# A chunked RWKV-7 inverse: accumulated in PSUM, transposed by VectorE in 32x32 blocks, two pairs' chains interleaved

## The chip, the cores and the metric

One core of a Trainium2 chip runs the whole program. The metric is the device time of one execution in microseconds; the times of before are the median of three runs with their lowest and highest. Lower is better.

## The reference

The program is one inference step of a two-layer hybrid decoder (D_MODEL 1024) in fp32, for one prompt of 256 tokens and eight samples of one token each. Each layer has a SwiGLU half (width 2816), a projection into three groups (RWKV-7, a short convolution, Mamba-2), a projection w_out back, and a second SwiGLU half. The change touches the RWKV-7 group alone. It has 16 heads of 64, and per token and head

```python
Sa = einsum('bhij,bhj->bhi', S, -kk_t)
S  = S * w_t[:, :, None, :] + Sa[..., None] * b_t[:, :, None, :] + v_t[..., None] * k_t[:, :, None, :]
y  = einsum('bhij,bhj->bhi', S, r_t)
```

The kernel does the prompt in four chunks of C = 64 tokens. Inside a chunk the coupling through Sa is a triangular system: with N the strictly lower 64x64 matrix of products between the tokens' b and kk vectors (each with its decay), X = (I - N)^-1 is needed for every head and chunk. The inverse is built by doubling: blocks of 2, and then for b in LEVELS = (2, 4, 8, 16, 32) the part of N that couples neighbouring blocks of size b, N_b, is taken in by X <- X + X N_b X. After level b, X consists of blocks of 2b on the diagonal.

## The kernel before

The eight samples and the prompt's tokens lie together as 264 columns. FFN and projection products stream weights from HBM, split in a high and a low fp32r half by ScalarE and VectorE or GpSimd (`Stream`, lines 154 to 236), three products per piece on TensorE.

`back_stage` (line 1574) holds the recurrence, w_out and the second FFN. It handles the 16 heads as RT = 8 pairs. A pair's four chunks of two heads are a tile of 128 partitions (two halves of 64) x 4 x 64. For a pair p the steps are:

- `decays` (ScalarE) and `weigh` (GpSimd, four multiplications) make the operands; `gram` (TensorE, line 2170) multiplies them into PSUM banks 3 and 4; `mask` (VectorE, line 1996) masks them into `gm`; `turn` and `tokens` bring transposed operands.
- `first` on GpSimd (line 1759) takes the first level out of gm into `xt`, the transpose of X; `start` (VectorE, line 2002) adds the identity. `turn_x` (TensorE, line 2192) multiplies it by the identity into PSUM bank 0, and `x_copy` (ScalarE, line 1809) makes `x` of it.
- Five levels i. `level` (GpSimd, line 1731) cuts N_b out of gm. `level_t1` (TensorE) forms N_b X in bank 0, `t1_copy` (ScalarE) brings it to `t1`, and `level_u` (TensorE) forms two products: X N_b X (bank 1, for levels 0 to 3) and its transpose (bank 2). `update` (VectorE, line 2007) adds the first to x and the second to xt, with x in SBUF. Each product is `blocks` (line 2186): eight matrix products of 64x64, sixteen instructions.
- `gv`, `solve` (line 2236, needs the finished xt), `transfer`, `own_outputs`, `own_states` and `chunk` carry the state through the four chunks; `mean_of`, `variance_of`, `centre`, `gated` normalise.
- `step(m, 0..7)` on VectorE does the recurrence of the eight samples for pair m; its rows come by DMA from `row_scratch`, its state by SyncE's queue.

Every engine has its own hand-written order in a loop `for g in range(RT + 2)`; all meet through counting semaphores. In a round g before, pair g gets gram, masks, start and turn_x; pair l = g - 1 gets all five levels, one behind the other; pair c = g - 2 gets solve, transfer, outputs and states; pair p = g - 3 gets its normalisation. Between the levels stand the other pairs' steps as filling. In rounds 8 and 9 the filling is the w_out product of the convolution groups, `short(mt)`: 24 products each; ScalarE there does the splits of w_out (`ws.split_hi`) and in round 8 the logarithm and exponential of five variances, with table loads. ScalarE also issues the stores of the final states (line 1838) and of the shift rows. VectorE has fillings too: in rounds 0 to 3 two bonus operations each (line 2112), in rounds 0 and 1 three and five scalings (line 2117). SyncE loads and stores the samples' rows and states and, from pair 6 on, w_out.

Of the kernel before, what the change touches and what calls it, by code (L numbers as in the profile page):

```python
# [22 lines left out]
P = 128  # L23
# [1550 lines left out]
def back_stage(nc, env, mix, layer, d):  # L1574
# [15 lines left out]
    with Stage(nc, f"back{layer}") as st:  # L1590
# [15 lines left out]
        t1 = st.sb("n_x", [P, 4, C])  # L1606
# [28 lines left out]

        def load_row(e, m, n):
# [4 lines left out]
        T1B, UB, GB, WB, EB = 0, 1, 3, 5, 6  # L1641
# [30 lines left out]
        with nc.Block() as block:  # L1672
# [42 lines left out]
            def _(pool):  # L1715
# [15 lines left out]
                def level(p, i):  # L1731
                    n = LV * p + i
# [18 lines left out]
                for g in range(RT + 1):  # L1751
                    l = g - 1
                    if l >= 0:
                        level(l, 1)
# [6 lines left out]
                    if l >= 0:  # L1761
                        level(l, 2)
                    if g + 1 < RT:
                        weigh(g + 1)
                    if l >= 0:
                        level(l, 3)
                    if g == RT - 1:
                        for q in range(3):
                            short_split_lo(q)
                    if g == RT:  # L1770
                        ws.split_lo(pool, 2)
                    if l >= 0:
                        level(l, 4)
                        key_row(l)
                    if g == RT - 1:
                        short_split_lo(3)
                    if g < RT:
                        level(g, 0)
# [7 lines left out]
            def _(act):  # L1786
# [15 lines left out]
                def t1_copy(p, i):  # L1802
                    n = LV * p + i
                    act.wait_ge(s("t1_ps"), n + 1)
                    if n:
                        act.wait_ge(s("ut_ps"), n)
                    act.activation(t1[:].rearrange("p q t -> p (q t)"), ps[:, T1B, 0:4 * C], ACT.Copy).then_inc(s("t1_in"), 1)  # L1807
# [73 lines left out]
                for i in range(2):  # L1881
                    act.activation(rows[0:V * NS].rearrange("p v b j -> p (v b j)")[:, i * 512:(i + 1) * 512],
                                   ps[0:V * NS, UB + i, :], ACT.Copy).then_inc(s("turned"), 1)
                act.activation(cend[:], mix.cum[:, :, :, C], ACT.Exp, scale=-DECAY).then_inc(s("cend"), 1)
                act.wait_ge(s("cend"), 1)
                for g in range(RT + 2):
                    l, c, p = g - 1, g - 2, g - 3
                    if g + 1 < RT:
                        decays(g + 1)
                    if 0 <= l < RT:  # L1890
                        t1_copy(l, 0)
                    if g == 1:
                        shift_rows(3)
                    if c >= 0:
                        uw_copy(c)
                    if c >= 1:
                        final_copy(c - 1)
                    if g == RT:
# [4 lines left out]
                    if g == RT + 1:  # L1903
                        ws.split_hi(act, 4)
                        ws.split_hi(act, 5)
                    if 0 <= l < RT:
                        t1_copy(l, 1)
# [4 lines left out]
                    if g < RT:  # L1912
                        tokens(g, 0)
                    if g < 2:
# [6 lines left out]
                    if 0 <= l < RT:  # L1921
                        t1_copy(l, 2)
# [3 lines left out]
                    if p >= 0:  # L1926
                        square(p)
                    if g == RT + 1:
                        ws.split_hi(act, 6)
                    if c >= 0:  # L1930
                        state_copy(c, 0)
                    if 0 <= l < RT:
                        t1_copy(l, 3)
# [3 lines left out]
                    if g < RT:  # L1937
                        tokens(g, 1)
                    if g == RT:
                        ws.split_hi(act, 3)  # L1940
                    if p >= 0:
                        variance(p)
                    if c >= 0:
                        state_copy(c, 1)
                    if 0 <= l < RT:
                        t1_copy(l, 4)
                        rv_copy(l)
# [9 lines left out]
                    if g < RT:  # L1957
                        x_copy(g)
# [36 lines left out]
            def _(dve):  # L1995
# [11 lines left out]
                def update(p, i):  # L2007
                    four = lambda b: ps[:, b, 0:4 * C].rearrange("p (q t) -> p q t", q=4)
                    if i < LV - 1:
                        dve.wait_ge(s("u_ps"), (LV - 1) * p + i + 1)  # L2010
                        if i:
                            dve.wait_ge(s("x_up"), (LV - 1) * p + i)
                        else:
                            dve.wait_ge(s("x_in"), p + 1)
                        dve.tensor_tensor(x[:, p % 2], x[:, p % 2], four(UB), ALU.add).then_inc(s("x_up"), 1)
                    dve.wait_ge(s("ut_ps"), LV * p + i + 1)
                    if i:
                        dve.wait_ge(s("xt_up"), LV * p + i)
                    dve.tensor_tensor(xt[:, p % 3], xt[:, p % 3], four(UB + 1), ALU.add).then_inc(s("xt_up"), 1)
# [62 lines left out]

                for g in range(RT + 2):
                    l, c, p = g - 1, g - 2, g - 3
                    if g < RT:
                        mask(g, 0)
                        mask(g, 1)
                    if 0 <= l < RT:
                        update(l, 0)
                        step(l, 0)  # L2090
# [4 lines left out]
                    if 0 <= l < RT:  # L2095
                        update(l, 1)
                        step(l, 1)
                        step(l, 2)
                        update(l, 2)
# [412 lines left out]
```

## Time and profile before

| | us |
|---|---|
| median of 3 runs | 1666.39 (1666.23 to 1671.9) |
| span of the profiled execution | 1667.1 |
| TensorE busy | 1566.2 |
| VectorE, ScalarE, GpSimd busy | 1140.1, 858.5, 262.7 |
| gram(0) to the last state copy, layer 0 | 441.2 to 597.0 |

The profiled execution's own time is its span, 0.7 us above the median. TensorE's busy time counts each matrix product to its modelled end, so products that wait for one another in a pipeline look like full work. In the windows below the columns are the stretch, its length, the busy time of TensorE (PE), its weight loads (PEld), VectorE (DVE), ScalarE (ACT) and GpSimd (POOL) with numbers of records, the granted TensorE clock (1.00 is 2.4 GHz), the DMA engines' busy share and GB/s. A timeline row is start, length, engine, line, operation, output and inputs, count, and in brackets the idle time before it with what ended it.

### The profile page before, as it was taken

Reading aid. Unit: us, or ns where it says so; the run is one execution under the profiler, and the core shown is the slowest. Engines: PE = TensorE matmul, PEld = TensorE weight load, DVE = VectorE, ACT = ScalarE, POOL = GpSimd, SP = SyncE. Lnnn points to the kernel's source line nnn. Section 1 sums busy time; section 2 is a strip of 40 time slices with the busy share of each in tenths; the row PEclk is TensorE's granted clock in tenths of the full one; section 3 lists DMA queues with packets and bytes.
Section 4 is the critical chain, followed back from the end, with each engine's and each line's share of the span. In section 5 each row is a group of like instructions: output and inputs, shape, how many; then the busy total and the mean of one; then the engine's idle time right before and its main releaser. Section 6 shows DMA issues by size and latency. Waiting matters only on the chain. (4 is left out here: it accounts for less than half of the span.)

```text
span 1667.1 us, 41414 instructions
## 1 busy us (share of the span) xinstructions
PE 1566.2 (94%) x17379; PEld 1486.8 (89%) x17379; DVE 1140.1 (68%) x1822; ACT 858.5 (51%) x1515; POOL 262.7 (16%) x259
## 2 busy tenths in 40 slices
PE   7999999989799899999999999999997989899997
PEld 6999999987688789999999999989775878799997
DVE  6565587795798667665575656968768886676654
ACT  5444464667444555444354444657673445554443
POOL 0000003001356431000000000030014554300000
PEclk9999999999899999999999999999998999999999
DMA  7555556471244545555454655644703463455552
GB/s 230 178 172 170 168 159 199 130 208 53 59 125 120 144 157 161 194 179 186 143 186 160 194 183 175 189 141 128 215 1 102 126 178 98 131 189 187 183 178 71
DMA packets 280650, 256.28 MB, mean 154 GB/s; under 512 B 48054, under 2 KB 268700, under 8 KB 280450
## 3 DMA queue, kind: packets, MB, share of 16 engines
q1 hardware_dynamic: 276698, 252.05, 48.5%
q8 instruction: 139, 2.28, 0.6%
q10 hardware_dynamic: 3768, 1.59, 0.4%
q14 instruction: 45, 0.37, 0.1%
HBM read 242.22 MB, written 11.38 MB: 152 GB/s over the span
## 5 line engine op out<-in xcount | busy, mean ns | idle before, releaser
L209 ACT ACTIVATE front_hi<-front_raw 128x1024 fp32r<-128x1024 f32 (+2 forms) x230 | 238.5, 1039 | 262.0 <-PE ps L234 255.5
L216 DVE TENSOR_TENSOR front_lo<-front_raw,front_hi 128x1024 fp32r<-128x1024 f32 (+1 forms) x210 | 252.2, 1201 | 109.0 <-ACT front_hi L209 108.2
L209 ACT ACTIVATE out_hi<-out_raw 128x1024 fp32r<-128x1024 f32 (+1 forms) x168 | 173.3, 1038 | 219.1 <-PE ps L234 205.1
L216 DVE TENSOR_TENSOR out_lo<-out_raw,out_hi 128x1024 fp32r<-128x1024 f32 (+1 forms) x148 | 183.9, 1243 | 108.1 <-ACT out_hi L209 107.3
L232 PE MATMUL ps<-front_h_hi,front_hi 128*128 128x264 f32 (+1 forms) x816 | 241.3, 296 | 4.9 <-DVE front_lo L216 3.3
L234 PE MATMUL ps<-front_h_hi,front_lo 128*128 128x264 f32 (+1 forms) x816 | 233.0, 286 | 0.0
L233 PE MATMUL ps<-front_h_lo,front_hi 128*128 128x264 f32 (+1 forms) x816 | 232.7, 285 | 0.0
L232 PE MATMUL ps<-ffn_h_hi,out_hi 128*128 128x264 f32 x704 | 200.7, 285 | 0.1
L233 PE MATMUL ps<-ffn_h_lo,out_hi 128*128 128x264 f32 x704 | 200.0, 284 | 0.0
L234 PE MATMUL ps<-ffn_h_hi,out_lo 128*128 128x264 f32 x704 | 199.8, 284 | 0.0
L232 PE MATMUL ps<-in_h_hi,front_hi 128*128 128x264 f32 x688 | 197.4, 287 | 0.0
L234 PE MATMUL ps<-in_h_hi,front_lo 128*128 128x264 f32 x688 | 196.5, 286 | 0.0
L233 PE MATMUL ps<-in_h_lo,front_hi 128*128 128x264 f32 x688 | 196.5, 286 | 0.0
L232 PEld LDWEIGHTS ps<-front_h_hi,front_hi 128*128 128x128 f32 (+1 forms) x816 | 154.1, 189 | 13.5 <-issue 12.7
L233 PEld LDWEIGHTS ps<-front_h_lo,front_hi 128*128 128x128 f32 (+1 forms) x816 | 154.2, 189 | 0.7
L234 PEld LDWEIGHTS ps<-front_h_hi,front_lo 128*128 128x128 f32 (+1 forms) x816 | 153.5, 188 | 0.1
L216 POOL TENSOR_TENSOR front_lo<-front_raw,front_hi 128x1024 fp32r<-128x1024 f32 (+1 forms) x20 | 50.1, 2504 | 543.9 <-ACT front_hi L209 543.9
L232 PEld LDWEIGHTS ps<-ffn_h_hi,out_hi 128*128 128x128 f32 x704 | 132.7, 189 | 0.4 <-ACT ffn_h_hi L283 0.2
L233 PEld LDWEIGHTS ps<-ffn_h_lo,out_hi 128*128 128x128 f32 x704 | 132.7, 188 | 0.1
L234 PEld LDWEIGHTS ps<-ffn_h_hi,out_lo 128*128 128x128 f32 x704 | 132.6, 188 | 0.0
L233 PEld LDWEIGHTS ps<-in_h_lo,front_hi 128*128 128x128 f32 x688 | 131.3, 191 | 0.1
L232 PEld LDWEIGHTS ps<-in_h_hi,front_hi 128*128 128x128 f32 x688 | 131.2, 191 | 0.1
(400 smaller groups left out, 3891.7 us busy)
## 6 DMA issues: line engine op xcount, KB each, us to landing
front_raw<-in_w_in SPq DMA_DIRECT2D x50, 1024.0 KB, 5.2
out_raw<-in_ffn_w_in SPq DMA_DIRECT2D x44, 1024.0 KB, 5.2
front_raw<-in_ffn_w_in SPq DMA_DIRECT2D x40, 1024.0 KB, 5.3
back_sample_rows<-row_scratch SPq DMA_DIRECT2D x160, 128.0 KB, 3.0
out_raw<-in_w_out SPq DMA_DIRECT2D x16, 1024.0 KB, 6.3
front_raw<-in_ffn_w_out SPq DMA_DIRECT2D x16, 896.0 KB, 4.6
out_raw<-in_ffn_w_out SPq DMA_DIRECT2D x16, 896.0 KB, 4.6
front_raw<-in_ffn_w_out SPq DMA_DIRECT2D x8, 1024.0 KB, 5.0
```

The costliest lines, as they stand in the source:

```text
L209: act.activation(self.hi[n % self.RING][:, 0:k, 0:w], self._raw(n), ACT.Copy).then_inc(self.hi_ready, 1)
L216: eng.tensor_tensor(self.lo[n % self.RING][:, 0:k, 0:w], self._raw(n), self.hi[n % self.RING][:, 0:k, 0:w].bitcast(F32), ALU.subtract).the ...
L232: pe.matmul(out, hi[:, j, 0:w], x_hi[:, j], start=start and j == 0, stop=False)
L233: pe.matmul(out, hi[:, j, 0:w], x_lo[:, j], start=False, stop=False)
L234: mm = pe.matmul(out, lo[:, j, 0:w], x_hi[:, j], start=False, stop=stop and j == k - 1)
```

## The change

1. X is accumulated in PSUM. `turn_x` starts an accumulation in bank 1 or 2 (by the pair's parity) and leaves it open; `level_u` of levels 0 to 3 adds X N_b X there, and `x_copy(p, i)` copies the bank to `x` before each level. The additions to x on VectorE are gone.
2. xt for levels 1 to 4 is `dve.transpose` of x, in 32x32 blocks. The second product of `level_u` is left for level 4 alone; one addition (`finish`) takes it into xt.
3. Levels 0, 1 and 2, 3, 4 of neighbouring pairs share a round: in round g pair g does levels 0 and 1, and pair b = g - 1 levels 2, 3 and 4, in the order (b,2) (g,0) (b,3) (g,1) (b,4) on TensorE. `t1` has two buffers.
4. start and turn_x stand at the beginning of pair g's own round; gram and masks of pair g + 1 towards its end, behind (b,4). The other steps are set into new places. Ahead of the loops stand gram(0), its masks and the first three shift turns.

```diff
-                def update(p, i):
-                    four = lambda b: ps[:, b, 0:4 * C].rearrange("p (q t) -> p q t", q=4)
-                    if i < LV - 1:
-                        dve.wait_ge(s("u_ps"), (LV - 1) * p + i + 1)
...
-                        dve.tensor_tensor(x[:, p % 2], x[:, p % 2], four(UB), ALU.add).then_inc(s("x_up"), 1)
-                    dve.wait_ge(s("ut_ps"), LV * p + i + 1)
...
-                    dve.tensor_tensor(xt[:, p % 3], xt[:, p % 3], four(UB + 1), ALU.add).then_inc(s("xt_up"), 1)
+                def turn_blocks(p, i):
+                    flat = lambda a: a.rearrange("p q t -> p (q t)")
+                    dve.wait_ge(s("x_in"), copied[p, i])
+                    dve.transpose(flat(xt[:, p % 3]), flat(x[:, p % 2])).then_inc(s("xt_in"), 1)
+
+                def finish(p):
+                    dve.wait_ge(s("u_ps"), order_of[p, 4] + 1)
+                    dve.tensor_tensor(xt[:, p % 3], xt[:, p % 3], ps[:, XB + p % 2, 4 * C:8 * C].rearrange("p (q t) -> p q t", q=4),
+                                      ALU.add).then_inc(s("xt_up"), 1)
...
-                def x_copy(p):
-                    act.wait_ge(s("x_ps"), p + 1)
-                    act.activation(x[:, p % 2].rearrange("p q t -> p (q t)"), ps[:, T1B, 0:4 * C], ACT.Copy).then_inc(s("x_in"), 1)
+                def x_copy(p, i):
+                    if i:
+                        act.wait_ge(s("u_ps"), order_of[p, i - 1] + 1)
+                    else:
+                        act.wait_ge(s("x_ps"), p + 1)
+                    act.activation(x[:, p % 2].rearrange("p q t -> p (q t)"), ps[:, XB + p % 2, 0:4 * C], ACT.Copy).then_inc(s("x_in"), 1)
...
+                def level_u(p, i):
+                    n = order_of[p, i]
+                    pe.wait_ge(s("t1_in"), n + 1)
                     if i:
+                        pe.wait_ge(s("xt_in"), turned_blocks(p, i))
+                    if i < LV - 1:
+                        blocks(XB + p % 2, 0, xt[:, p % 3], t1[:, n % 2], False, i == LV - 2).then_inc(s("u_ps"), 1)
                     else:
...
+                        blocks(XB + p % 2, 4 * C, t1[:, n % 2], xt[:, p % 3]).then_inc(s("u_ps"), 1)
```

TensorE's order in a round after the change, from the diff (b = g - 1, c = g - 2, p = g - 3): t1(b,2), solve(c), turn_final(c-1), [short(2)], turn_x(g), u(b,2), t1(g,0), turn(g,0), [short(0)], transfer(c), mean_of(p), u(g,0), t1(b,3), turn(g,1), own_outputs(c), u(b,3), t1(g,1), own_states(c), variance_of(p), [short(1)], u(g,1), t1(b,4), chunk(c,1), gram(g+1), gv(b), chunk(c,2), u(b,4), chunk(c,3). The shorts are those of rounds 8 and 9.

VectorE's: start(g), turn_blocks(b,3), step(b,0), transfer(c), turn_blocks(g,1), step(b,1), centre(p), step(b,2), turn_blocks(b,4), step(b,3), gated(p), turn_blocks(g,2), fillings, step(b,4), mask(g+1) twice, step(b,5), finish(b), step(b,6), step(b,7).

ScalarE's: t1_copy(b,2), uw_copy(c), final_copy(c-1) with its store, x_copy(g,0), x_copy(b,3), decays(g+1), t1_copy(g,0), [shift rows 0 to 2 in round 0], tokens(g,0), x_copy(g,1), [shift store], t1_copy(b,3), tokens(g,1), square(p), x_copy(b,4), t1_copy(g,1), state_copy(c,0), variance(p), x_copy(g,2), t1_copy(b,4), the other state copies. In round 8 the logarithm block stands behind x_copy(b,3).

GpSimd's: first(g), level(g,0), level(b,3), weigh(g+1), level(g,1), [short splits in round 7], level(b,4), key_row(b), level(g,2).

## Rows read from the trace of the kernel before

**Rows 1.** The page, part 1: busy time, share of the span, instructions.
```profile
PE 1566.2 (94%) x17379; PEld 1486.8 (89%) x17379; DVE 1140.1 (68%) x1822; ACT 858.5 (51%) x1515; POOL 262.7 (16%) x259
```

**Rows 2.** Windows of layer 0: length, busy us (records) by engine, clock, DMA share, GB/s.
```profile
450.45:467.31 16.86, 13.95 (x335) 11.97 (x335) 15.52 (x28) 6.42 (x18) 8.86 (x11) 1.00 0.38 124
...
497.24:511.64 14.40, 14.05 (x426) 12.57 (x424) 13.29 (x26) 6.58 (x20) 9.17 (x11) 1.00 0.48 134
...
543.90:562.02 18.12, 14.23 (x409) 12.71 (x406) 13.45 (x25) 8.65 (x24) 10.85 (x10) 1.00 0.96 270
...
562.02:582.87 20.85, 18.52 (x420) 16.77 (x416) 12.33 (x22) 13.09 (x22) 9.86 (x7) 1.00 0.11 31
...
467.31:543.90 76.59, 72.50 (x2164) 65.64 (x2160) 67.17 (x123) 33.84 (x99) 45.52 (x55) 1.00 0.45 125
```

**Rows 3.** Timeline of two half levels, layer 0, fifth round.
```profile
514.03 0.68 PE L2189 MATMUL ps<-back_inverse,back_n_levels 64*64 64x64 f32 x16
...
514.44 0.64 ACTq L1838 DMA_DIRECT2D out_p_wkv<-back_final_state  x1
...
515.18 0.38 ACT L1807 ACTIVATE back_n_x<-ps 128x256 f32<-128x256 f32 x1 [0.77 <-PE ps L2189]
...
515.61 0.68 PE L2189 MATMUL ps<-back_n_x,back_inverse_t 64*64 64x64 f32 x16 [0.36 <-ACT back_n_x L1807]
...
516.13 0.63 PE L2189 MATMUL ps<-back_inverse_t,back_n_x 64*64 64x64 f32 x16
```

**Rows 4.** Waits of 449 to 600 us: total us, times, longest us.
```profile
ACT back_n_x L1807 <- PE ps L2189: 21.5, 26, 2.7
...
PEld ps L2189 <- issue: 9.0, 18, 2.9
```

**Rows 5.** Groups by line over the span: xcount | busy us, mean ns | idle before.
```profile
L2189 PE MATMUL ps<-back_inverse,back_n_levels 64*64 64x64 f32 x1280 | 54.3, 222 | 7.5 <-issue 6.2 <-ACT back_inverse L1811 0.7
...
L2189 PE MATMUL ps<-back_inverse_t,back_n_x 64*64 64x64 f32 x1280 | 53.1, 220 | 3.3 <-issue 3.2
...
L2189 PE MATMUL ps<-back_n_x,back_inverse_t 64*64 64x64 f32 x1024 | 44.0, 225 | 9.4 <-ACT back_n_x L1807 9.1
...
L2019 DVE TENSOR_TENSOR back_inverse_t<-back_inverse_t,ps 128x256 f32<-128x256 f32 x80 | 33.4, 418 | 7.1 <-PE ps L2189 4.7
...
L1807 ACT ACTIVATE back_n_x<-ps 128x256 f32<-128x256 f32 x80 | 30.5, 381 | 45.6 <-PE ps L2189 44.8
...
L2015 DVE TENSOR_TENSOR back_inverse<-back_inverse,ps 128x256 f32<-128x256 f32 x64 | 26.8, 419 | 26.4 <-PE ps L2189 25.8
...
L1871 ACT ACTIVATE shift_new_rows<-ps 9x512 f32<-9x512 f32 (+1 forms) x14 | 7.7, 564 | 2.4 <-PE ps L2345 2.0
```

**Rows 6.** Timeline of VectorE, two additions back to back.
```profile
498.43 0.41 DVE L2015 TENSOR_TENSOR back_inverse<-back_inverse,ps 128x256 f32<-128x256 f32 x1
498.76 0.41 DVE L2019 TENSOR_TENSOR back_inverse_t<-back_inverse_t,ps 128x256 f32<-128x256 f32 x1
```

**Rows 7.** Timeline, start of the stage in layer 0.
```profile
443.25 1.29 DVE L1998 TENSOR_TENSOR back_products<-ps,cst 128x512 f32<-128x512 f32 x2 [5.15 <-PE ps L2182]
...
446.33 0.68 PE L2198 MATMUL ps<-cst,back_inverse_t 64*64 64x64 f32 x16 [0.23 <-DVE back_inverse_t L2004]
```

**Rows 8.** Timeline of the eighth round, layer 0.
```profile
565.47 0.37 PE L232 MATMUL ps<-short_hi,out_hi 128*128 128x264 f32 x1
...
566.68 1.28 ACT L1900 ACT_TABLE_LOAD   x1 [0.66 <-ACT back_final_state L1836]
...
570.69 1.31 ACT L1860 ACTIVATE xs<-xs 128x1320 f32<-128x1320 f32 x1
...
571.29 0.28 PE L234 MATMUL ps<-short_hi,out_lo 128*128 128x264 f32 x1
```

**Rows 9.** Line 2039 on VectorE: shortest, median, longest ns.
```profile
L2039 DVE TENSOR_TENSOR back_prod<-back_sample_wkv,back_sample_rows x16: 684/980/1267, 452.5 to 1388.1; 128x512 f32<-128x512 f32 x16
```

**Rows 10.** Windows of TensorE ahead of the stage, clock in the last but two columns.
```profile
436.00:438.00 2.00, 0.01 (x1) 0.50 0.00 0
```

More of the change, by code:

```diff
@@ L1634, in back_stage, with turned_blocks @@
         M0, R0, G0, Y0 = 0, P, 2 * P, 3 * P
+        order_of = {}
+        for g in range(RT + 1):
+            order = [(g - 1, 2), (g, 0), (g - 1, 3), (g, 1), (g - 1, 4)]
+            for pair, i in order:
+                if 0 <= pair < RT:
+                    order_of[pair, i] = len(order_of)
+        copied = {}
+        for g in range(RT + 1):
+            for pair, i in [(g, 0), (g - 1, 3), (g, 1), (g - 1, 4), (g, 2)]:
+                if 0 <= pair < RT:
+                    copied[pair, i] = len(copied) + 1
+        def turned_blocks(p, i):
+            return sum(1 for (pair, j), n in copied.items() if j and n <= copied[p, i])
         def load_row(e, m, n):
@@ L1777, in _ @@
                     if g < RT:
-                        level(g, 0)
+                        level(g, 2)
                     if g == RT - 1:
@@ L1895, in _ @@
                         uw_copy(c)
+                    if g == RT + 1:
+                        ws.split_hi(act, 4)
+                        ws.split_hi(act, 5)
                     if c >= 1:
                         final_copy(c - 1)
+                    if g < RT:
+                        x_copy(g, 0)
+                    if 0 <= b < RT:
+                        x_copy(b, 3)
+                    if g and g + 1 < RT:
+                        decays(g + 1)
                     if g == RT:
@@ L2081, in y_split_lo @@
                     dve.tensor_tensor(y_lo[:, p], r[:, p], y_hi[:, p].bitcast(F32), ALU.subtract).then_inc(s("y_lo"), 1)
+                mask(0, 0)
+                mask(0, 1)
                 for g in range(RT + 2):
-                    l, c, p = g - 1, g - 2, g - 3
+                    b, c, p = g - 1, g - 2, g - 3
                     if g < RT:
[L2086 to L2090, printed above, removed]
+                        start(g)
+                    if 0 <= b < RT:
+                        turn_blocks(b, 3)
+                        step(b, 0)
                     if g == RT + 1:
@@ L2108, in _ @@
                     if g < RT:
-                        start(g)
+                        turn_blocks(g, 2)
                     if g < 4:
@@ L2118, in _ @@
                                                  op0=ALU.mult, op1=ALU.mult).then_inc(s("short_scaled"), 1)
-                    if 0 <= l < RT:
-                        step(l, 5)
-                        update(l, 4)
-                        step(l, 6)
-                        step(l, 7)
+                    if 0 <= b < RT:
+                        step(b, 4)
+                    if g + 1 < RT:
+                        mask(g + 1, 0)
+                        mask(g + 1, 1)
+                    if 0 <= b < RT:
+                        step(b, 5)
+                        finish(b)
+                        step(b, 6)
+                        step(b, 7)
                     if g == RT - 1:
@@ L2184, in gram, with blocks @@
                     mm.then_inc(s("g_ps"), 1)
-                def blocks(at, left, right):
+                def blocks(bank, at, left, right, start=True, stop=True):
                     for q in range(4):
                         for w in half:
-                            mm = pe.matmul(ps[w, at, q * C:(q + 1) * C], left[w, q], right[w, q], start=True, stop=True)
+                            mm = pe.matmul(ps[w, bank, at + q * C:at + (q + 1) * C], left[w, q], right[w, q], start=start, stop=stop,
+                                           skip_group_check=not start)
                     return mm
@@ L2400, in _ @@
                         shift_turn(6)
-                    if 0 <= l < RT:
-                        level_t1(l, 3)
-                    if g < RT:
-                        turn(g, 1)
                     if p >= 0:
                         variance_of(p)
-                    if 0 <= l < RT:
-                        level_u(l, 3)
+                    if g == RT:
+                        short(1)
+                    if g < RT:
+                        level_u(g, 1)
+                    if 0 <= b < RT:
+                        level_t1(b, 4)
                     if c >= 0:
                         chunk(c, 1)
-                    if 0 <= l < RT:
-                        level_t1(l, 4)
-                        gv(l)
+                    if g + 1 < RT:
+                        gram(g + 1)
+                    if 0 <= b < RT:
+                        gv(b)
                     if g == RT + 1:
```

197 lines of the change are left out of this document (92 added, 105 removed).

## The prediction

> **What bounds the kernel now.** I read the page first: TensorE is busy for 94% of the span [rows 1], so only a stretch in which it waits, or works for nothing, can give time. The windows then show where the changed code runs: some 156 us of either layer, from the first gram products (441.2 us in layer 0) to the last state copy. I cut layer 0 at the starts of the mask products (line 1998, pairs 1, 2 and 7) and of the solve products (line 2243, pairs 6 and 7) [rows 2]. From mask 2 to mask 7 lie five equal rounds of 15.3 us; TensorE shows 72.5 us of 76.6 and VectorE 67.2. Neither is as full as it looks: TensorE's 64x64 products count long tails as busy (sixteen records are 0.68 us busy, but the next sixteen begin 0.52 us behind them [rows 3]). VectorE is the one that is really near full: 13.29 of 14.40 us in the round from 497.24 [rows 2].
>
> The waits of the stretch say what the order of a round is made of: ScalarE waits 21.5 us for the inverse's products, and TensorE loses 9.0 us to its own instruction supply [rows 4]. The timeline gives the step of the chain: product to copy, copy to product. A product takes 0.68 us till its data can be read; from the start of a copy to the next product 0.43 us pass [rows 3]. So half a level is 1.11 us, a level 2.2 us, and five in a row 11.1 us of a 15.3 us round, with other pairs' work in between.
>
> **The change part by part**, layer 0, then doubled. The profiled execution has a span of 1667.1 us, 0.7 above the median of 1666.4; I take differences from the first and set them on the second.
>
> *Removed on TensorE.* Of the 14 block calls of a pair four go (u transposed in levels 0 to 3): 64 instructions, 32 calls in a layer. By [rows 3] a call occupies 0.52 us from start to start, so up to 16.6 us a layer. That is worth its price only where TensorE is the last; see the first rival.
>
> *VectorE.* Nine additions from PSUM per pair (64 and 80 in two layers, [rows 5]) become four block transpositions and one addition. Back to back, additions begin 0.33 us apart though each lasts 0.41 [rows 6]. No row shows a transposition. From below: half an addition, one source in place of two, 0.2 us. From above: twice one, 0.85, since 32 columns must be in before one can leave. I take the addition's 0.33 apart (0.42 long), the nearest row of that size. So a round loses four times 0.33, less little for filling: 1.24 us. The Trainium skill (VectorE: DVE Perf Modes, The three transpose paths) gives 311 ns for a 128x128 bf16 block transposition on VectorE; with 128 more columns at its 0.96 GHz that is an estimate of 444 ns, which would leave this sum where it is. No row shows it yet.
>
> *ScalarE.* Per pair four more copies of X at 0.38 us [rows 5], 1.5 us. ScalarE is busy for 34 of 77 us in the rounds [rows 2], so as work this is free. As an order it is not: a copy of X stands behind the store of the final state, whose issue holds the queue for 0.64 us [rows 3].
>
> *Order.* In a round VectorE now ends with: masks of the next pair, step 5, the closing addition, steps 6 and 7, then start. Behind start TensorE must turn the new X, and the product that stood behind the turn goes to ScalarE before VectorE can transpose: turn and product 0.5 us each, 0.68 till readable, and behind the store's issue a copy of 0.4: VectorE idles 1.5 us there. It idles some 0.3 us more for the transfer products (step 0 fills most of that) and 0.4 for X of the other pair (u and its copy, 1.1 us, beside two transfer additions). I take 2.2 us of waits a round.
>
> - Five rounds, mask 2 to mask 7: VectorE's work 67.2 - 5 x 1.24 = 61.0 us, waits 5 x 2.2 = 11.0, together 72.0 against 76.6: **-4.6**. TensorE's calls fit: some 13 us of start to start a round. A supply stall now falls mostly into waits; I add nothing for it.
> - Round 0. Before, mask 1 stood at 450.45, 7.2 us behind mask 0 [rows 2, 7]. Now gram 1 comes after both levels of pair 0, and mask 1 after the second transposition and the filler of round 0. From the turn of X at 446.33 [rows 7]: five half levels of 1.11 (turn, two levels) 5.5 us; in their way on ScalarE three row copies of 0.56 [rows 5] and a store, 2.0; transposition 0.35; then two bonus and three scaling operations at 0.42, 2.1. Mask 1 stands at 456.3: **+5.8**.
> - Round 1, mask 1 to mask 2: VectorE's 15.52 us [rows 2] less 1.24, with 2.2 of waits: 16.5 against 16.9, **-0.4**.
> - Round 7, mask 7 to solve 6: 18.1 us before, 2.9 of it the longest stall of [rows 4]. Now GpSimd's last level products stand behind its short splits, and those behind ScalarE's splits, which have X copies in front; GpSimd's 10.85 us of work [rows 2] get late by about what the chain gained. I take 0, between -3 and +2.
> - Round 8, solve 6 to solve 7: 20.9 us with all five levels of pair 7, products of w_out between them (5.9 us for two groups, [rows 8]) and on ScalarE the logarithm and exponential block from 566.68 to 572.0 [rows 8]. Two of five levels are gone, done a round earlier beside pair 6: 4.4 us by the step above, and 0.3 for the second group that now stands further back. **-4.1**.
>
> Sum: +5.8 - 0.4 - 4.6 + 0 - 4.1 = -3.3 us a layer, -6.6 in all; 1667.1 - 6.6 = 1660.5 for the profiled execution, **1660 us** as a median. All behind it is a stream of w_out and FFN products with the same work, so the stage's end moves the kernel's end one to one. Single bounds: waits of a round 1.2 to 3.2, 5 us a layer either way; transposition 0.2 to 0.85 long, -7 to +14 a layer (4 x 8 calls).
>
> **The rivals.**
>
> *The chains no longer bind and the engines' savings arrive.* For it: ScalarE's 21.5 us of waiting are all at the chain, which falls from five levels in a row to three, and TensorE had only 4 us visibly free in 76.6. Against it: VectorE is the fuller one, and start, turn, copy, transposition is a new loop across three engines. If the waits of a round shrink to 0.7: 7 rounds x 1.5 = 10.5 us a layer more; 1660 - 21 = **1639**.
>
> *Slower: the transposition's price.* One mechanism: VectorE has four of them a round in a loop that it closes itself (masks, steps, start, transpose), so each nanosecond above my price counts 32 times a layer. The forecast's 6.6 us are used up at 64 x 0.10, that is from 0.52 us for one on. At 0.85 us it is 64 x 0.43 = 27 us: **1687**; at 0.75, 1681. For it: VectorE operations of this stage that share SBUF with GpSimd last 0.98 in the median where the fastest takes 0.68 [rows 9], and a transposition reads and writes SBUF alone, where the addition had one PSUM source. Against it: only 256 columns.
>
> *The fill eats all.* In round 1 TensorE waits for start of pair 1 behind the filler, some 4 us idle. Its clock was at 0.50 (1.2 GHz) at 436 to 438 us, in the idle time behind the front stage [rows 10]; should it fall to that level again here, products of round 1 take twice as long, and with late shift rows on ScalarE that is 3 us a layer: **1667**, no change. The Trainium skill (TensorE: Matmul & The Clock Gate, Part 1) says that the throttled clock is the default and activity releases it, a rule that speaks against any new gap; the row of 0.50 agrees.
>
> *It doesn't do what it says:* a transposition in 32x32 blocks is X's transpose only while X has no entries outside them. The last level used is 32, and X before it is made of 32x32 blocks; the fifth level keeps its product. So it holds.
>
> **How the numbers follow.** Forecast 0.45, alone 1648 to 1672 (the waits' bounds); free chains 0.22; dear transposition 0.22; fill 0.11. To tell it from no change takes about 0.5%, 8.3 us: below 1658 or above 1675. Faster: 0.4 of the forecast's 0.45 and all of 0.22, 0.40. Slower: 0.23. Same: the rest, 0.37. Range: 1638 to 1683, which takes in most of both outer cases.
>
> **What would show it.** The turn of X (line 2198) is late against gram: mask 1 some 6 us later after mask 0, mask 2 to mask 7 near 72 us, solve 6 to solve 7 near 17. In the groups the transposition at 0.42 us; VectorE's idle time put down to ScalarE's copies of X. Wrong it would be if a transposition lasts over 0.52 us, if the five rounds take under 68 or over 76 us, or if round 8 keeps its 20.9.

## The result, and the profile after

The changed kernel takes 1680.3 us (median; 1676.12 to 1680.37, 4 runs), the kernel before 1668.1 (1666.23 to 1671.9, 4 runs): a ratio of 1.0069, 95% interval 1.0049 to 1.0089. It is slower by 12 us, where 6.4 us faster was forecast. The profiled execution of after is its fastest run: 1676.12 us, span 1674.1, 7.0 above the span of before. A span is some 2 us shorter than the time of its own run, so the profiled execution of before took some 1669.1 us (an estimate: 1667.1 + 2.0), 1.0 above its median, and not 1667.1 as the section on the time before has it. The 12.2 us between the medians are these 7.0, that 1.0, and 4.2 by which after's other three runs are longer than its profiled one. The traces below explain the 7.0; of the other runs there is no trace.

The engines' work did fall, against [rows 1]: VectorE by 31 us, TensorE's records by 16 us and 1024 instructions; ScalarE's rose by 23 and GpSimd's by 9.

```profile
PE 1550.2 (93%) x16355; PEld 1463.3 (87%) x16355; DVE 1108.9 (66%) x1758; ACT 881.6 (53%) x1579; POOL 271.7 (16%) x259
```

The new operation costs about what was put down for it: it lasts 0.44 us (0.42 forecast), and the next operation begins 0.37 us behind its start (0.33). Behind it on the line stands the idle time of VectorE ahead of it, 63.6 us where the additions had 26.4 and 7.1 [rows 5]:

```profile
L2038 DVE STREAM_TRANSPOSE back_inverse_t<-back_inverse 128x256 f32<-128x256 f32 x64 | 28.4, 444 | 63.6 <-ACT back_inverse L1829 63.1
```

So the work is gone and the time is not. The windows of layer 0, cut at the same instructions as [rows 2] (masks are line 2026 now, solve line 2275), say where; the first runs from mask 0 to mask 1, then mask 2, mask 7, solve 6, solve 7:

```profile
442.62:455.00 12.38, 8.57 (x156) 6.67 (x154) 5.01 (x10) 5.22 (x14) 5.52 (x8) 0.97 0.66 167
455.00:471.49 16.49, 11.72 (x239) 10.41 (x239) 10.38 (x21) 7.32 (x19) 9.06 (x11) 0.79 0.25 69
471.49:549.85 78.36, 68.58 (x1806) 59.03 (x1808) 58.76 (x104) 40.94 (x117) 47.76 (x55) 0.93 0.43 118
549.85:569.80 19.95, 15.46 (x403) 12.84 (x399) 15.28 (x23) 11.97 (x33) 13.16 (x11) 1.00 0.87 246
569.80:587.31 17.51, 15.05 (x285) 13.17 (x285) 11.73 (x17) 12.41 (x22) 9.23 (x5) 1.00 0.33 80
```

Against before the five stretches give +5.2, -0.4, +1.8, +1.8 and -3.3 us, in all +5.1; in layer 1 the same cuts give +5.7, -0.4, 0.0, -0.7 and -3.7, +0.9. The remaining 1.0 us lies outside the stage. In the middle stretch of layer 0 set the busy time of TensorE (68.58) and of VectorE (58.76) against the length: TensorE was idle for 9.8 us by its records where it was 4.1, VectorE for 19.6 where it was 9.4, and the granted clock was 0.93 where it was 1.00.

What the engines wait for in these five rounds, the "full rounds" (471.49 to 549.85; who waits, behind the arrow for whom; total us, times, longest us):

```profile
POOL back_inverse_t L1772 <- DVE back_products L2026: 17.5, 5, 4.9
POOL back_b_k L1744 <- ACT back_decays L1806: 14.4, 5, 3.4
DVE back_inverse_t L2038 <- ACT back_inverse L1829: 14.3, 12, 2.5
...
PE ps L2275 <- DVE back_inverse_t L2042: 5.3, 4, 3.8
PE ps L2230 <- DVE back_inverse_t L2032: 4.8, 5, 1.0
```

GpSimd waited for the masks before too. The other four are new, or were under 2 us: the transposition waits for a copy of X, TensorE waits for the closing addition (2042) and for start (2032), GpSimd for ScalarE's decays. In [rows 4] the long wait was ScalarE's for the inverse's products.

Some full rounds are alike to 0.02 us (14.96 to 14.98, one in layer 0 and three in layer 1): the text calls them undisturbed, and they show the loop. This is 519.32 to 534.29, the first half, with the other engines' rows that belong to it (DVE is VectorE, ACT ScalarE; in brackets the idle time ahead):

```profile
519.32 1.29 DVE L2026 TENSOR_TENSOR back_products<-ps,cst 128x512 f32<-128x512 f32 x2 [0.17 <-PE ps L2211]
520.52 0.68 DVE L2076 TENSOR_TENSOR back_sample_wkv<-back_sample_wkv,back_outer 128x512 f32<-128x512 f32 x1
521.12 0.41 DVE L2042 TENSOR_TENSOR back_inverse_t<-back_inverse_t,ps 128x256 f32<-128x256 f32 x1
521.45 0.89 DVE L2079 TENSOR_TENSOR back_prod<-back_sample_wkv,back_sample_rows 128x512 f32<-128x512 f32 x1
522.37 0.69 DVE L2081 TENSOR_REDUCE xs<-back_prod 128x8 f32<-128x512 f32 x1
522.98 0.91 DVE L2032 TENSOR_TENSOR back_inverse_t<-back_inverse_t,cst 128x256 f32<-128x256 f32 x1
523.94 0.68 PE L2230 MATMUL ps<-cst,back_inverse_t 64*64 64x64 f32 x16 [1.03 <-DVE back_inverse_t L2032]
524.67 0.85 ACT L1829 ACTIVATE back_inverse<-ps 128x256 f32<-128x256 f32 x2 [1.19 <-PE ps L2230]
525.55 0.45 DVE L2038 STREAM_TRANSPOSE back_inverse_t<-back_inverse 128x256 f32<-128x256 f32 x1 [1.67 <-ACT back_inverse L1829]
...
527.12 0.42 DVE L2049 TENSOR_TENSOR back_carry<-ps,cst 128x256 f32<-128x256 f32 x1 [0.54 <-PE ps L2299]
...
528.76 0.45 DVE L2038 STREAM_TRANSPOSE back_inverse_t<-back_inverse 128x256 f32<-128x256 f32 x1 [0.89 <-ACT back_inverse L1829]
```

Start begins 3.66 us after the masks, behind three steps of the sample state that no product of the inverse needs. TensorE idles 1.03 us for it, with the older pair's next product and all the new pair's queued behind the turn; then VectorE idles 1.67 us for the answer. Two engines wait for each other in one loop, and the round lasts 14.97 us, of which 3.27 are VectorE's waits.

### The profile page after: what moved, and what is told of

It is laid out like the page before. It is cut to its first block and busy times, and to the rows that moved or that the text cites. A ratio compares the mean times of both kernels' runs of the same rounds, so it can differ in the third digit from the quotient of the medians.

```text
span 1674.1 us, 39220 instructions
## 1 busy us (share of the span) xinstructions
PE 1550.2 (93%) x16355; PEld 1463.3 (87%) x16355; DVE 1108.9 (66%) x1758; ACT 881.6 (53%) x1579; POOL 271.7 (16%) x259
## 5 line engine op out<-in xcount | busy, mean ns | idle before, releaser
L216 DVE TENSOR_TENSOR out_lo<-out_raw,out_hi 128x1024 fp32r<-128x1024 f32 (+1 forms) x148 | 179.7, 1214 | 106.2 <-ACT out_hi L209 105.4
```

The lines of the kernel that those rows point to most:

```text
L216: eng.tensor_tensor(self.lo[n % self.RING][:, 0:k, 0:w], self._raw(n), self.hi[n % self.RING][:, 0:k, 0:w].bitcast(F32), ALU.subtract).the ...
```

## The experiments

Ten kernels ran, each beside the kernel before on the same chip (its medians there 1667.3 to 1668.7); a ratio is to that one, with its 95% interval in brackets. "after" is the changed kernel, 1680.3, whose four runs stand with the result and were not repeated beside these. Differences from it are by the medians; by the ratios they are smaller: 7.5, 13.8 and 20.7 us for the three kernels below that are given 9, 16 and 22.6. The code cuts are shortened.

### Which half of the change costs: order or products

The rounds of before, with X summed in PSUM, copied by ScalarE and turned by VectorE (VectorE's part):

```diff
-                    if i < LV - 1:                 # before's update: two additions
-                        dve.tensor_tensor(x, x, u, add)
-                    dve.tensor_tensor(xt, xt, ut, add)
+                    if i < LV - 1:
+                        dve.transpose(flat(xt), flat(x))
+                    else:
+                        dve.tensor_tensor(xt, xt, ut, add)
```

> Before's order of the rounds (five levels of one pair in a row, gram at the head of a round), with the inverse accumulated in PSUM and transposed by VectorE. Theory 1 (the order of the new rounds costs the time: VectorE's closing steps, the addition, start and the turn form one loop of some 15.5 us and TensorE idles in it): with the old order the four fewer block calls and the 1.2 us less of VectorE a round are a gain, 3 to 8 us a layer, so 1652 to 1662 us. Theory 2 (the new products cost the time: a copy by ScalarE, in its queue, stands between two levels where VectorE's addition stood, and the transposition waits for it): 1675 us or more, with ScalarE's copies of X the longest wait.

1662.9 us (1661.28 to 1666.79, 11 runs), ratio 0.9977 [0.9968, 0.9986], 0.9 above theory 1's range. And the other half, the new order with before's products and additions:

```diff
-    blocks(XB + p % 2, 0, xt, t1, False, i == LV - 2)
+    blocks(UB, xt, t1); blocks(UB + 1, t1, xt)      # and update() as before
```

> The new order of the rounds, with before's two products and two additions a level. Theory 1 (order): the rounds stay at 15.5 us or grow by VectorE's 1.2 us each, first rounds as slow as in the changed kernel: 1680 to 1695 us. Theory 2 (products): the interleaving alone is harmless or a gain, 1655 to 1668 us.

1697.3 us (1695.75 to 1701.18, 4 runs), ratio 1.0184 [1.0169, 1.0198], 2.3 above theory 1's range. The new way of making the inverse gains some 4 us in the old order and 17 in the new one; the order costs 17 with the new products and 30 with the old. The 30 hold more than the order: there the two pairs' products share banks 1 and 2, and each waits for the other pair's addition. Either way what is wrong with after is in its order. The five rounds of layer 0 in these two, the old order first:

```profile
466.49:542.33 75.84, 65.80 (x1846) 57.76 (x1842) 58.45 (x103) 41.03 (x119) 46.68 (x55) 0.98 0.45 126
```
```profile
472.21:556.46 84.25, 75.13 (x2126) 66.50 (x2128) 68.04 (x124) 33.73 (x97) 46.49 (x55) 0.96 0.40 110
```

In the old order VectorE's work is 58.5 us, the same as in after, and 8.7 us less than before buy 0.75 us; in layer 1 the five rounds lasted 78.1 us, with one of 17.3 among them (76.1 before; this profiled execution is the kernel's slowest run). So less work of VectorE did not shorten the round of before. I read its five-level chain as the limit; that is argued and not shown, since the same edit puts a copy and a transposition into each level in place of the additions.

### Is it the loop through start

Start stands at the head of the next round in after; here it moves ahead of steps 6 and 7, and the closing addition ahead of step 5.

```diff
                 mask(0, 0)
                 mask(0, 1)
+                start(0)
                 for g in range(RT + 2):
                     b, c, p = g - 1, g - 2, g - 3
-                    if g < RT:
-                        start(g)
...
                         mask(g + 1, 1)
                     if 0 <= b < RT:
+                        finish(b)
                         step(b, 5)
-                        finish(b)
+                    if g + 1 < RT:
+                        start(g + 1)
+                    if 0 <= b < RT:
                         step(b, 6)
                         step(b, 7)
```

> The changed kernel; VectorE's order at the end of a round is masks, closing addition, step 5, start of the next pair, steps 6 and 7, instead of masks, step 5, addition, steps 6 and 7, start. Theory 1 (loop through start): the turn of X comes 1.5 to 2 us earlier in every round, VectorE's steps 6 and 7 fill the wait for ScalarE's copies of X; rounds 14.0 to 14.5 us, the clock stays up, 1655 to 1668 us. Theory 2 (products): same work, other order, within 3 us of 1680.

1671.0 us (1669.07 to 1674.19, 9 runs), ratio 1.0024 [1.0014, 1.0033]: 9 us off after, and 3 above the upper end of theory 1's range. Undisturbed rounds fall to 13.9 to 14.0 us in layer 1 (14.97 in after), the five to 71.2 (76.07 in after), but only to 76.2 in layer 0 (78.36).

```profile
1297.18:1368.38 71.20, 66.26 (x1806) 57.29 (x1808) 63.10 (x103) 40.96 (x117) 47.94 (x55) 0.95 0.45 128
```

VectorE's busy time rose from 59.0 to 63.1 with the same operations, since some now begin behind one of GpSimd's and not ahead of it (last section; shown there for step 5, which lasts 0.4 us longer a round, of 0.8 in all).

### Is it what stands ahead of the masks in the first rounds

The bonus and scaling operations of the first four rounds ("fillers") stood behind the newer pair's last transposition, so ahead of the next masks. In the second round of after, TensorE waits for start of pair 1 behind them; the fillers of that round stand ahead of the third masks, and behind those TensorE waits for the closing addition of pair 0:

```profile
453.02 0.86 DVE L2136 SCALAR_TENSOR_TENSOR bonus<-bonus,cols,gate 128x264 f32<-128x264 f32 x2
453.79 1.30 DVE L2141 SCALAR_TENSOR_TENSOR y_short<-y_short,cols,sc_root 128x264 f32<-128x264 f32 x3
455.00 1.28 DVE L2026 TENSOR_TENSOR back_products<-ps,cst 128x512 f32<-128x512 f32 x2
...
458.12 1.12 PE L2230 MATMUL ps<-cst,back_inverse_t 64*64 64x64 f32 x16 [3.61 <-DVE back_inverse_t L2032]
...
473.76 1.72 PE L2275 MATMUL ps<-back_gv_a,back_inverse_t 64*64 64x128 f32 x16 [3.76 <-DVE back_inverse_t L2042]
```

In the edit `fillers(g)` stands for the two loops of these operations:

```diff
                     if g < RT:
                         start(g)
+                    fillers(g)                     # bonus and scaling, rounds 0 to 3
                     if 0 <= b < RT:
                         turn_blocks(b, 3)
...
                         turn_blocks(g, 2)
-                    fillers(g)
```

> The changed kernel with one edit: VectorE's bonus and scaling operations of the stage's first four rounds stand ahead of the block transposition of the older pair's fourth level instead of behind that of the newer pair's third. In the changed kernel they stand between the chain of the first pair and the second pair's masks, so that the first round lasts 12.4 us against 7.2 us. Theory A (what is in front of the masks on VectorE costs in rounds 0 and 1): the first two rounds give 2 to 3 us a layer back, 4 to 6 us in all, 1674 to 1677 on the scale where the changed kernel has 1680. Theory B (the first round is bound by the chain of transposition, copies and products alone, and the fillers fit into its waits): within 2 us of the changed kernel.

1664.4 us (1661.89 to 1668.82, 12 runs), ratio 0.9986 [0.9977, 0.9995]: 16 us off after, about three times what was expected. This one edit turns the loss into a small gain. Mask 1 and mask 2 come 11.0 and 14.7 us after their predecessors in layer 0 (12.4 and 16.5), 10.5 and 13.3 in layer 1 (12.9 and 16.5); and the five rounds too lose 3.7 and 1.4 us. That is, together, 13.8 of the 14.0 us between the two spans. TensorE waits 1.75 us for start in the second round, not 3.61:

```profile
456.44 0.68 PE L2230 MATMUL ps<-cst,back_inverse_t 64*64 64x64 f32 x16 [1.75 <-DVE back_inverse_t L2032]
```
```profile
453.33:468.05 14.72, 11.32 (x223) 9.25 (x221) 11.36 (x19) 7.10 (x18) 9.69 (x11) 0.88 0.22 69
...
468.05:542.68 74.63, 66.28 (x1852) 56.79 (x1850) 59.83 (x102) 42.08 (x120) 48.50 (x55) 1.00 0.45 126
```

Five rounds of 14.97 would be 74.85: with the fillers out of the way three of the five in layer 0 and four in layer 1 last 14.96 to 14.98 us, in layer 0 at a granted clock of 1.00. What is left is the loop.

### Do GpSimd's late weights cost anything

```diff
                     if c >= 1:
                         final_copy(c - 1)
+                    if g and g + 1 < RT:
+                        decays(g + 1)
                     if g < RT:
                         x_copy(g, 0)
                     if 0 <= b < RT:
                         x_copy(b, 3)
-                    if g and g + 1 < RT:
-                        decays(g + 1)
```

> The changed kernel with one edit: ScalarE computes the two decays of the next pair ahead of the copies of X, not behind the older pair's copy. GpSimd waits 33.1 us in both layers for them in the changed kernel. Theory A (GpSimd's levels are late and hold the products of a chain): the full rounds lose 0.3 to 0.6 us each, 1671 to 1677. Theory B (GpSimd's wait is slack; the loop of masks, start, turning and steps 6 and 7 sets the round): within 2 us of 1680, or up to 3 us slower, since each copy of X stands 0.7 us later.

1677.6 us (1675.68 to 1678.29, 6 runs), ratio 1.0060 [1.0047, 1.0073], which its interval does not part from after's 1.0069; the median lies between the two theories' ranges. GpSimd's wait fell as meant, from 33.1 us over the span to

```profile
POOL back_b_k L1744 <- ACT back_decays L1806: 13.6, 10, 1.6
```

and the steady rounds of layer 1 lasted 15.1 us, not 14.97. A wait of 14.4 us in the list of the five rounds, the longest of the new ones, was slack.

### The edits together

> The changed kernel with three edits together: the next pair's start ahead of steps 6 and 7, the decays ahead of the copies of X, and the fillers ahead of the fourth level's transposition. If the three costs stand beside each other (9 us measured for the start alone, 4 to 6 for the fillers, 0 to 4 for the decays): 1660 to 1667, at or just below the kernel before at 1667. If the start's move already took what the others would give (one chain behind another): 1669 to 1672 as with the start alone.

1664.1 us (1658.56 to 1668.78, 12 runs), ratio 0.9979 [0.9967, 0.9990]: inside the range for costs that stand beside each other, but only since the fillers' share in it was put at 4 to 6. Together the three edits bring no more than the fillers' alone. The full rounds of layer 1 last 14.6 us, where with start alone they lasted 13.9: once start is early, ScalarE's two decays (0.72 us) ahead of the copy of X are in the loop.

> The changed kernel with two edits: the start ahead of steps 6 and 7, and the fillers ahead of the fourth level's transposition; the decays stay where the changed kernel has them. With the fillers alone the five full rounds lasted 74.6 and 74.7 us (15.0 each), with the start alone 76.2 and 71.2 (13.9 each at the end of layer 1), with all three edits 76.4 and 71.9 (14.6 each). Theory A (the loop start, turning, copy, transposition, level sets the full round, and the decays ahead of the copy of X lengthened it by 0.6 us): full rounds of 13.9 to 14.3 in layer 1, 1658 to 1662 in all. Theory B (the fillers' move took from the same slack as the start's): full rounds as with the fillers alone, 1663 to 1666.

So the decays went back to where after has them. 1657.7 us (1653.79 to 1662.15, 6 runs), ratio 0.9945 [0.9930, 0.9960]: theory A, 0.3 below its range, and the best of all; 9.6 us faster than before and 22.6 than after. The five rounds of both layers:

```profile
467.50:538.72 71.22, 65.95 (x1852) 56.65 (x1849) 62.59 (x102) 42.05 (x120) 48.58 (x55) 1.00 0.48 134
1283.45:1353.28 69.83, 65.12 (x1852) 56.31 (x1850) 62.75 (x103) 42.08 (x120) 48.67 (x55) 1.00 0.47 131
```

and the loop in one of them, to be read beside the round of after above:

```profile
1325.32 1.29 DVE L2026 TENSOR_TENSOR back_products<-ps,cst 128x512 f32<-128x512 f32 x2
1326.53 0.41 DVE L2042 TENSOR_TENSOR back_inverse_t<-back_inverse_t,ps 128x256 f32<-128x256 f32 x1
1326.86 1.12 DVE L2076 TENSOR_TENSOR back_sample_wkv<-back_sample_wkv,back_outer 128x512 f32<-128x512 f32 x1
1327.89 0.94 DVE L2032 TENSOR_TENSOR back_inverse_t<-back_inverse_t,cst 128x256 f32<-128x256 f32 x1
1328.76 1.21 DVE L2079 TENSOR_TENSOR back_prod<-back_sample_wkv,back_sample_rows 128x512 f32<-128x512 f32 x1
1328.89 0.68 PE L2232 MATMUL ps<-cst,back_inverse_t 64*64 64x64 f32 x16 [0.48 <-DVE back_inverse_t L2032]
...
1330.61 0.43 DVE L2038 STREAM_TRANSPOSE back_inverse_t<-back_inverse 128x256 f32<-128x256 f32 x1
```

Start begins 2.57 us after the masks (3.66 in after), TensorE waits 0.48 us (1.03), and VectorE reaches the transposition without idling (1.67): steps 6 and 7 fill the time of the turn and the copy. The gain of the stage is larger than that of the kernel: from mask 0 to solve 7 it lasts 133.7 and 132.6 us against 139.6 and 141.7 before, 15.0 less, while the span is 10.8 less. Another 1.0 us comes ahead of the first mask, and 5.2 go again behind the stages (2.4 after layer 0's, 2.8 after layer 1's); what takes them stays open.

> The two edits of the kernel with start and fillers moved, and one more: in the first round ScalarE copies the three shift rows behind the copies of the tokens and of X, not ahead of them. Theory A (in the first round the copies for the new chain wait behind the shift rows' 1.5 us): the first round falls by 0.5 to 1.2 us in each layer, 1 to 2 us in all. Theory B (the X copy waits for TensorE's product, which is late itself behind the token transpositions): no difference, or up to 1 us slower, since the shift banks come free later for TensorE's next shift rows.

1660.0 us (1654.67 to 1665.96, 7 runs), ratio 0.9954 [0.9936, 0.9972], not parted from the one before it. Theory A named the first round: it lasted 10.6 us in layer 1 (11.0 without the edit) but 11.4 in layer 0 (10.5). The second lasted 13.3 in both (14.7), at a granted clock of 1.00 (0.88); but 13.3 is also what it lasted in layer 1 of the kernel with the fillers alone, which does not have this edit. So the edit's worth is not shown. The stage of layer 1 was 2.0 us shorter (130.6), that of layer 0 3.0 longer (136.7): four full rounds lasted 14.7 to 15.8 us there. Such long rounds at full clock are in three of the four early-start kernels, in layer 0 only. In the one with all three edits, 513.45 to 546.49, TensorE's list reads

```profile
PE ps L2220 <- issue: 2.6, 2, 1.3
PE ps L2338 <- issue: 1.6, 2, 0.9
PE ps L2324 <- issue: 1.1, 2, 0.9
```

that is, it waited for nothing that the profile shows. This is open.

### Does the clock cost anything of its own

In after, TensorE's granted clock fell to 0.50, its lower level of 1.2 GHz, from 457.0 to 463.8 us and again from 474.1 to 480.9, each time in or just behind one of the long waits shown above; a third fall in layer 0, from 508.2 to 511.6, stood behind waits of 0.93 us for the closing addition and 1.03 for start. Sixteen turning products took 1.12 us there where they take 0.68 at 1.00 (458.12 and 523.94 above).

```profile
457.20:463.60 6.40, 5.49 (x84) 5.04 (x84) 1.98 (x4) 2.64 (x7) 3.83 (x6) 0.50 0.08 15
```

Spare products on the same engine ahead of the two waits of every round; `spare(bank, n)` is n products of constants that nobody reads:

```diff
+                    if p:
+                        spare(XB + p % 2, 6 if p == 1 else 1)    # turn_x
+                    if p < RT - 1:
+                        spare(WB, 6 if p == 0 else 2)            # solve
```

> The changed kernel with spare 128x128x256 fp32 products of constants, whose result nobody reads, ahead of the two waits in which TensorE idles in a round (six in rounds 1 and 2, else two ahead of solve and one ahead of the turn of X; in idle time for the most part). Theory 1a (the fall of the clock to 0.50 behind those waits costs about 1.5 us a time, in two to three rounds a layer): 4 to 8 us less than the changed kernel's 1680, so 1672 to 1676, rounds 1 and 2 below 15.5. Rival (the waits alone cost it, the clock follows and is hidden by them): no change or slower by what the spare products delay, 1680 to 1686.

1682.5 us (1679.33 to 1684.4, 6 runs), ratio 1.0086 [1.0072, 1.0100], whose interval overlaps after's [1.0049, 1.0089]. The clock was kept in the two rounds that had lost it, and they lasted 15.8 and 14.9 us (16.5 and 16.0). In layer 0 the five rounds lasted 75.9 us, 2.5 less than in after; in layer 1 they lasted 78.3, 2.3 more, and the round behind them 24.05 (20.20):

```profile
456.39:472.17 15.78, 13.31 (x256) 11.28 (x255) 10.47 (x21) 7.26 (x19) 9.06 (x11) 1.00 0.24 73
472.17:487.07 14.90, 13.09 (x352) 11.15 (x351) 11.85 (x21) 6.83 (x19) 9.71 (x11) 1.00 0.39 99
...
1313.09:1376.51 63.42, 60.02 (x1492) 49.45 (x1489) 47.15 (x83) 34.01 (x99) 38.82 (x44) 1.00 0.43 119
```

So once more, with spare products (six each) at the first pair's solve and the second pair's turn alone:

> The changed kernel with six spare products of TensorE (into a bank that the next products overwrite) ahead of two waits only: the second pair's turning and the first pair's solve. The full rounds have none. With spare products ahead of every such wait the second to fourth masks came after 15.8 and 14.9 us (16.5 and 16.0 in the changed kernel) with the granted clock at 1.00, but the later rounds lasted 15.2 to 16.4 and the time did not fall. Theory A (the half clock in the second and third round costs time of its own): these rounds again last 15.8 and 14.9, the later ones 15.0 as in the changed kernel, 1676 to 1679 where the changed kernel has 1680. Theory B (the fall of the clock only fills waits that stand anyway): within 1 us of the changed kernel or above it, 1679 to 1682.

1678.3 us (1675.01 to 1679.9, 6 runs), ratio 1.0057 [1.0040, 1.0074]; its interval holds after's ratio. The median lies in theory A's range, and in layer 0:

```profile
455.92:471.70 15.78, 13.30 (x256) 11.27 (x255) 10.46 (x21) 7.27 (x19) 9.06 (x11) 1.00 0.24 73
471.70:486.68 14.98, 12.47 (x351) 10.90 (x349) 11.85 (x21) 6.85 (x19) 9.71 (x11) 1.00 0.34 94
486.68:503.50 16.82, 14.47 (x367) 12.40 (x364) 12.07 (x24) 8.28 (x25) 8.96 (x11) 0.90 0.43 118
```

The two rounds gain 1.8 us, the first loses 0.6, and the fourth takes 1.2 (15.6 in after), with the clock falling there instead. By the medians the clock is worth 2 us of the 12; the intervals do not exclude nothing, and the profiled execution, 1679.4 us, was 3.3 longer than after's. The clock followed the waits. The fillers' move, which shortened the waits, shortened its falls too (8 us of the stage of layer 0 at the half clock, 18 in after) and brought 14 to 16 us. The early start left them as long as they were (22 and 16 us in the two layers; 18 and 15 in after) and still took 7 to 9 us off.

## Why the prediction was wrong, step by step

- *Engines' work and the transposition's price* were right, or nearly. VectorE has 58.8 us of work in the five rounds; 61.0 were forecast, in part because each addition saved was counted at 0.33 us and is 0.41 of busy time. The transposition lasts 0.444 us (0.42 taken), so the rival of the dear transposition falls; that its 1681 for 0.75 us is the number nearest to the 1680.3 is chance. The Trainium skill (VectorE: DVE Perf Modes, The three transpose paths) gives 311 ns for the 128x128 bf16 block transposition; the prediction's estimate from it was 444 ns, and the trace agrees with it (444 ns in the mean of 64).
- *Five rounds, mask 2 to mask 7, "waits 5 x 2.2 = 11.0, together 72.0 against 76.6: -4.6"* is the step that failed. They lasted 78.4 us in layer 0 and 76.1 in layer 1, and VectorE waited 19.6 and 17.1 us, 3.9 and 3.4 a round. The waits were 8.6 us more than forecast in layer 0, and 2.2 us of work less hid part of it, which leaves an error of 6.4. It has two parts. An undisturbed round waits 3.3 us, so five take 74.9: 2.9 us. Each term of the 2.2 us was too small there: behind start 1.67 (1.5 forecast), for the transfer 0.54 (0.3), for the other pair's X 0.89 (0.4), for gram ahead of the masks 0.17 (nothing). I had the loop in hand and treated its wait as given: steps 5 to 7, which no product of the inverse needs, went into the sum as plain work, though ahead of start they hold TensorE too. The early start, which moves two of them behind it, shows that this could be had: with it a round takes 13.9 us, below the 14.4 forecast. The other 3.5 us are rounds disturbed by what came ahead of them: pair 0's solve 3.8 us late and a half clock. That these carried over from round to round is argued; that the fillers set them off is shown, since moving the fillers brought the stretch to 74.6.
- *Round 0, +5.8*: +5.2 and +5.7. The size was right, and I took as given what could be moved: the fillers (2.1 us of it) stood in the way of the masks.
- *Round 1, -0.4*: -0.4 in both layers, for a wrong reason. I had VectorE working 14.3 us and waiting 2.2; it worked 10.4 and waited 6.1. The number came right by chance, and hid that in this round the engines wait for each other.
- *Round 7, 0*: +1.8 and -0.7, inside its bounds. *Round 8, -4.1*: -3.3 and -3.7; two levels fewer are worth 3.5 us.
- *The fill rival* (1667, no change) came nearest in its mechanism: TensorE idled 3.6 us for start of pair 1 (I had said some 4) and its granted clock fell to 0.50. The Trainium skill (TensorE: Matmul & The Clock Gate, Part 1) says that the throttled clock is the default and activity releases it; the fall behind this wait agrees. The rival's size was too small since it stopped at round 1, where the delay went on into the full rounds. Its products at the half clock in round 1 are there (6.8 us of it), but keeping the clock gave this round only 0.7 us.
- *Free chains* (1639) falls: the chain of five levels was replaced by a loop, and only once that was shortened, and the fillers moved, did 5.4 and 6.3 us arrive in the five rounds.
- *Readings of the rows.* The 9.0 us of [rows 4] were called TensorE's own instruction supply; the row says only that its weight loads waited for nothing that the profile shows. The range of 1648 to 1672 is wider than its bound on the waits, 5 us a layer, which gives 1650 to 1670.

The prediction's test lines were the right ones: it said that over 76 us in the five rounds would prove it wrong, and they lasted 78.4 in layer 0; the 76.1 of layer 1 are what before had there, where 72 was forecast. By the profiled executions the terms now sum to +5.1, +0.9 and 1.0 outside the stage; why the other three runs of after are 4.2 us longer than the profiled one stays open.

## What to carry to other kernels

When a change breaks one long chain into two, find the new loop and write its members down in order on each engine: every operation ahead of the one that another engine waits for has its price in both queues, however small it is in the sum of busy time. Fill work belongs behind the operation that releases the other engine, where its time runs beside the answer; moving sixteen such operations a layer was worth 14 to 16 us here. And a sum of the form "work plus waits" that comes out right is checked only when both terms do.

## What the runs showed of the hardware

- VectorE turned 128x256 fp32 in 32x32 blocks, SBUF to SBUF, in 0.444 us, 0.03 more than an addition of that size from PSUM (0.41).
- Where step 5 of VectorE and GpSimd's first operation of a pair, both fp32 and between SBUF tensors, overlap, the one that begins second is stretched. Step 5 (line 2076) begins 0.17 us ahead of GpSimd's operation of line 1772 in after, and 0.17 us behind it in the kernel with start and fillers moved. Their GpSimd rows, after first, are to be read beside VectorE's rows of 520.52 and 1326.86: 0.68 and 1.10 us in after, 1.12 and 0.73 in the other. Over all 16 pairs the medians are 0.68 and 1.10, and 1.11 and 0.73.

```profile
520.69 1.10 POOL L1772 TENSOR_TENSOR back_inverse_t<-back_products,cst 128x256 f32<-128x256 f32 x1 [3.83 <-DVE back_products L2026]
```
```profile
1326.69 0.73 POOL L1772 TENSOR_TENSOR back_inverse_t<-back_products,cst 128x256 f32<-128x256 f32 x1 [2.56 <-DVE back_products L2026]
```

- Spare products kept TensorE's granted clock at 1.00 in rounds where it had been at 0.79, and no gain of the whole kernel is shown by it: 1678.3 us with them in two places and 1682.5 with them in every round, against 1680.3, with intervals that overlap.
